# Row norms of q and k summed on the token side, and their inverse spread by TensorE, in a two-block transformer kernel

## The chip, the cores and the metric

The kernel runs on one core of a Trainium2 chip. The metric is the time of one execution in microseconds on the device; lower is better. The core has a matrix engine (TensorE, PE in the rows), a vector engine (VectorE, DVE), an activation engine (ScalarE, ACT), a general engine (GpSimd, POOL) and a queue that issues transfers (SyncE, SP). Each runs its own program, and they meet at semaphores.

## The reference, cut to what matters

The program is a stack of two blocks of two layers each, on 256 tokens of width 1024, all in float32. The first block (attention, memory attention, gated feed-forward) is not touched. Each of the two layers of the second block has a mixer, and in the mixer a gated delta rule with four heads of 128. Its queries and keys are normalised per token and head:

```python
def _l2norm(x):
    return x * lax.rsqrt(jnp.sum(x * x, axis=-1, keepdims=True) + EPS)
...
    qkv = jax.nn.silu(_dwconv(qkv, dn_conv)).astype(f32)
    q, k, v = _split(qkv, (DN_WIDTH, DN_WIDTH, DN_WIDTH))
    q = _l2norm(_to_heads(q, DN_HEADS)) * (DN_HEAD_DIM ** -0.5)
    k = _l2norm(_to_heads(k, DN_HEADS))
```

That is 2 (q, k) x 4 heads x 256 tokens = 2048 sums, each over 128 features.

## The kernel before, in words

**The stream of weights.** All weights pass through a ring of three slots of 1 MB each ("units"). ScalarE rounds each half of a unit to a high part (`w_hi`, 128x1024), VectorE subtracts to get the low part (`ring_lo`), and TensorE multiplies each unit in three passes (high x high, high x low, low x high). `feed(u)` on ScalarE and VectorE is the pair of halves of unit u+2; ScalarE may write a half of `w_hi` only when TensorE is done with the same half of unit u.

**The PSUM tiles.** Results that are not accumulated over a whole stage go into four banks, in a fixed order of tiles (class `Plan`). Tile t uses bank t modulo 4, and TensorE opens it (`open_tile`) only when tile t-4 has been read out. A tile's reader raises `tile_taken` of its bank.

**The mixer of layer l** (`mixer2`, once in each engine's program). TensorE first runs 18 units of projections (`PROJECTED`): q, k, v come out with features on the partitions and tokens along the row, in `qkvT`, 12 slabs of 128x256, of which slabs 0 to 3 are the heads of q and 4 to 7 those of k. ScalarE squares slabs 0 to 7 into `l2s` while the projection `hi` runs. Between the last unit of `hz` and the first of `z`, TensorE sums the squares: four matmuls with a matrix of ones as the stationary operand and 512 columns of squares moving, so that every partition receives the sum (tiles `l2`, four of them). Then it sums the decays (`decay_sums`, tile `gcum`, line 1115). ScalarE turns each of the four tiles into a 128x512 inverse root with Ln (line 1676) and Exp (line 1680) after loading the table for the two (line 1672), and VectorE multiplies q and k by it (line 2383). The units of `z` pass through Silu (line 1598).

**The loop of nine levels** (`for k in range(LEVELS + 2)`) follows. On TensorE a turn has the level's attention (eight matmuls, in turn 0 sixteen; tiles `level`), something extra (`prepare(k)`), and for k < 8 one unit `gate` of 48 matmuls on 256 columns. The extra is: k=0 and 1 the rows of the decays (`gcB0`, `gcB1`, eight matmuls each), k=2 the transposes of k and v to tokens on the partitions (`kv_T`, 16 of them), k=3 the products k x k (`G`, eight matmuls), k=4 the products q x k (`QK`, eight matmuls). On VectorE a turn is `gather` (reads the two level tiles, L2310 or L2313), its own `prepare`, `qmul` (L2296), `args` (L2273 and L2275) and `feed` of the gate unit (L1785 twice). On ScalarE it is `level_exp` (L1608), its `prepare` (at k=0 and 1 the decay matrices, L1697 and L1704), `feed` of the gate unit (L1314 twice) and the copy of the gate tile (L1279).

The order of instructions on each engine is the order in which the code is written; nothing is reordered.

Of the kernel before, what the change touches and what calls it, by code (L numbers as in the profile page):

```python
# [29 lines left out]
ALU = mybir.AluOpType  # L30
# [3 lines left out]
P = 128  # L34
# [34 lines left out]
PREP.update({0: (("gcB0", 2),), 1: (("gcB1", 2),), 2: (("kv_T", 4),), 3: (("G", 2),), 4: (("QK", 2),)})  # L69


class Plan:
# [104 lines left out]
    def stages(self):  # L177
# [287 lines left out]
def build(nc, weights, x_in, mem_in, consts, cols, ln_g_rows, ln_b_rows, gains, sink, rpb, hmask_in, wba_in, head_rows, decay_rows, final_norm,  # L465
          out):
    plan = Plan()
    with ExitStack() as ctx:
# [60 lines left out]
        def table(name):  # L529
# [36 lines left out]
                  "l2_sq", "l2_inv", "l2_done",  # L566
# [39 lines left out]
        l2_eps, ngc = small[:, 14, 0:2], small[:, 16, :]  # L606
# [90 lines left out]
        def _(pe):  # L697
# [375 lines left out]
            def mixer2(l):  # L1073
# [51 lines left out]
                def prepare(k):  # L1125
                    if k in (0, 1):
                        decay_rows_of(k)
                    if k == 2:
                        pe.wait_ge(sems["l2_done"], 4 * l + 4)
# [3 lines left out]
                    if k in (3, 4):  # L1133
                        for tt in range(TT):
                            per_head(T[("G" if k == 3 else "QK", l)] + tt, lambda h: qkvT[:, 4 + h, tt * P:(tt + 1) * P],
                                     lambda h: qkvT[:, (4 if k == 3 else 0) + h, tt * P:(tt + 1) * P])
# [129 lines left out]
        def _(act):  # L1266
# [323 lines left out]
            def mixer2(l):  # L1590
# [78 lines left out]
                for j in range(2):  # L1669
                    feed_one("hz", j)  # L1670
                    silu_tokens(T[("hz", l, j)], tok2(hz, j))
# [9 lines left out]
                for j in range(2):  # L1681
                    feed_one("z", j)
                    silu_tokens(T[("z", l, j)], tok2(zs, j))

                def prepare(k):
# [19 lines left out]
                    if k == 2:  # L1705
# [62 lines left out]
        def _(dve):  # L1768
# [561 lines left out]
            def mixer2(l):  # L2330
# [40 lines left out]

                t = T[("gcum", l)]
# [7 lines left out]
                feed_one("z", 0)  # L2380
                for j in range(4):
                    dve.wait_ge(sems["l2_inv"], 4 * l + j + 1)
                    V.tensor_tensor(pair(qkvT, j), pair(qkvT, j), pair(l2s, j), ALU.mult).then_inc(sems["l2_done"], 1)
                feed_one("z", 1)

                def prepare(k):
                    if k == 1:
                        dve.wait_ge(sems["gc_exp"], l + 1)
                        V.scalar_tensor_tensor(nbe, beta, -1.0, eg, ALU.mult, ALU.mult).then_inc(sems["nbe"], 1)
                    if k == 3:  # L2390
# [15 lines left out]
                    if k == 4:  # L2406
# [151 lines left out]
            step.did(V.tensor_scalar(l2_eps[:, 0:1], ident[:, 0:1], 0.0, P * EPS, ALU.mult, ALU.add))  # L2558
            step.link(V.tensor_scalar(l2_eps[:, 1:2], ident[:, 0:1], 0.0, EPS, ALU.mult, ALU.add))
# [132 lines left out]
```

## Time and profile before

| | us |
|---|---|
| median of 3 executions (2355.98 to 2367.64) | 2361.45 |
| the profiled execution | 2361.45 |
| its span from first to last instruction | 2359.7 |
| TensorE busy in the span | 2256.3 (96%) |
| VectorE busy | 1573.7 (67%) |
| ScalarE busy | 1075.8 (46%) |
| GpSimd busy | 151.3 (6%) |

The span is the time between the first and the last recorded instruction. Times in rows of a timeline are microseconds from its start. The mixer of layer 0 begins at about 1269 us, that of layer 1 at about 1811 us. The granted TensorE clock was 1.00 of full speed (2.4 GHz) between 1346 and 1470 us and between 1880 and 2012 us, the stretches in which the change lies. A float32 matmul shows as two records, each with a weight load of its own; a transpose shows as one.

### The profile page before, as it was taken

Reading aid. Unit: us, or ns where it says so; the run is one execution under the profiler, and the core shown is the slowest. Engines: PE = TensorE matmul, PEld = TensorE weight load, DVE = VectorE, ACT = ScalarE, POOL = GpSimd, SP = SyncE. Lnnn points to the kernel's source line nnn. Section 1 sums busy time; section 2 is a strip of 40 time slices with the busy share of each in tenths; the row PEclk is TensorE's granted clock in tenths of the full one; section 3 lists DMA queues with packets and bytes.
Section 4 is the critical chain, followed back from the end, with each engine's and each line's share of the span. In section 5 each row is a group of like instructions: output and inputs, shape, how many; then the busy total and the mean of one; then the engine's idle time right before and its main releaser. Section 6 shows DMA issues by size and latency. Waiting matters only on the chain.

```text
span 2359.7 us, 40274 instructions
## 1 busy us (share of the span) xinstructions
PE 2256.3 (96%) x16242; PEld 2105.1 (89%) x16242; DVE 1573.7 (67%) x2370; ACT 1075.8 (46%) x1524; POOL 151.3 (6%) x141
## 2 busy tenths in 40 slices
PE   7999889999999999999998998999999999899997
PEld 7998869989999998889997998998998999898996
DVE  4557747665665575756557878667767778567766
ACT  4335555433443455554333674334344575234432
POOL 0000000221000000000000011500000010500000
PEclk9999989999999999999999999999999999899999
DMA  7554414575555553435553433014554443014553
GB/s 260 182 192 170 152 54 161 169 220 182 206 195 188 180 194 126 142 145 179 187 186 130 161 126 108 1 72 161 189 184 161 161 143 120 7 42 164 190 185 124
DMA packets 52669, 359.75 MB, mean 152 GB/s; under 512 B 6400, under 2 KB 6784, under 8 KB 10944
## 3 DMA queue, kind: packets, MB, share of 16 engines
q1 hardware_dynamic: 46928, 340.81, 40.7%
q0 software_dynamic: 4336, 13.37, 1.9%
q10 hardware_dynamic: 1280, 3.77, 0.5%
q8 instruction: 95, 1.56, 0.3%
q14 instruction: 30, 0.25, 0.0%
HBM read 356.88 MB, written 1.05 MB: 152 GB/s over the span
## 4 chain that ended last, share of the span: by engine, by line
PE 83%; DVE 8%; ACT 4%; DMA 3%; issue 1%; POOL 0%; SPq 0%; POOLq 0%; DVEq 0%; ACTq 0%
PE tile L736 43%; PE acc L769 19%; PE tile L749 7%; PE tile L1060 6%; DMA ring<-weights 3%; PE tile L1243 2%; DVE ring_lo L1785 2%; ACT w_hi L1314 2%; PE tile L905 1%; PE tile L879 1%; PE tile L784 1%; PE tile L892 1%; DVE work L2467 0%; DVE bn L2170 0%; PE tile L710 0%
## 5 line engine op out<-in xcount | busy, mean ns | idle before, releaser
L1785 DVE TENSOR_TENSOR ring_lo<-ring,w_hi 128x1024 fp32r<-128x1024 f32 x648 | 782.1, 1238 | 605.1 <-ACT w_hi L1314 602.5
L1314 ACT ACTIVATE w_hi<-ring 128x1024 fp32r<-128x1024 f32 x648 | 657.5, 1053 | 887.8 <-DMA ring<-weights 722.1
L736 PE MATMUL tile<-xT_hi,w_hi 128*128 128x256 f32 x3008 | 856.1, 285 | 20.2 <-DVE xT_lo L1776 13.9
L736 PE MATMUL tile<-xT_lo,w_hi 128*128 128x256 f32 x3008 | 852.6, 283 | 0.0
L736 PE MATMUL tile<-xT_hi,ring_lo 128*128 128x256 f32 x3008 | 852.6, 283 | 0.0
L736 PEld LDWEIGHTS tile<-xT_hi,w_hi 128*128 128x128 f32 x3008 | 578.6, 192 | 27.7 <-DVE ring_lo L1785 12.7
L736 PEld LDWEIGHTS tile<-xT_lo,w_hi 128*128 128x128 f32 x3008 | 578.7, 192 | 2.1
L736 PEld LDWEIGHTS tile<-xT_hi,ring_lo 128*128 128x128 f32 x3008 | 578.6, 192 | 0.0
L769 PE MATMUL acc<-w_hi,hidden_hi 128*128 128x512 f32 x528 | 206.7, 391 | 3.1 <-DVE ring_lo L1785 3.1
L769 PE MATMUL acc<-w_hi,hidden_lo 128*128 128x512 f32 x528 | 206.1, 390 | 0.0
L769 PE MATMUL acc<-ring_lo,hidden_hi 128*128 128x512 f32 x528 | 205.5, 389 | 0.0
L1060 PE MATMUL tile<-work 128*128 128x128 f32 (+1 forms) x1568 | 191.5, 285 | 14.2 <-DVE work L2445 5.8
L1060 PEld LDWEIGHTS tile<-work 128*128 128x128 f32 x1568 | 187.8, 200 | 17.0 <-issue 9.3
L1279 ACT ACTIVATE work<-tile 128x512 f32<-128x512 f32 (+2 forms) x206 | 113.1, 570 | 128.4 <-PE tile L1060 87.9
L769 PEld LDWEIGHTS acc<-w_hi,hidden_hi 128*128 128x128 f32 x528 | 99.3, 188 | 23.0 <-issue 3.5
L769 PEld LDWEIGHTS acc<-ring_lo,hidden_hi 128*128 128x128 f32 x528 | 99.1, 188 | 21.1
L769 PEld LDWEIGHTS acc<-w_hi,hidden_lo 128*128 128x128 f32 x528 | 99.4, 188 | 18.3
L749 PE MATMUL tile<-w_hi,xT_hi 128*128 128x256 f32 x352 | 100.2, 285 | 7.2 <-ACT work L1585 3.2
L749 PE MATMUL tile<-w_hi,xT_lo 128*128 128x256 f32 x352 | 99.6, 283 | 0.0
L749 PE MATMUL tile<-ring_lo,xT_hi 128*128 128x256 f32 x352 | 99.6, 283 | 0.0
L2636 POOL TENSOR_TENSOR work<-work,levels 128x512 f32<-128x512 f32 x56 | 69.0, 1257 | 174.2 <-PE tile L1060 164.4
L769 PE MATMUL acc<-w_hi,xT_hi 128*128 128x512 f32 x192 | 77.6, 404 | 0.0
(254 smaller groups left out, 2681.9 us busy)
## 6 DMA issues: line engine op xcount, KB each, us to landing
ring<-weights SPq DMA_DIRECT2D x324, 1024.0 KB, 4.8
work<-ln_g_rows POOLq DMA_DIRECT2D x8, 512.0 KB, 5.0
work<-ln_b_rows POOLq DMA_DIRECT2D x8, 512.0 KB, 5.8
work<-rpb POOLq DMA_DIRECT2D x32, 96.0 KB, 14.3
work<-hmask_in ACTq DMA_DIRECT2D x1, 1408.0 KB, 9.8
x<-x_in SPq DMA_DIRECT2D x1, 1024.0 KB, 7.9
work<-mem_in ACTq DMA_DIRECT2D x1, 1024.0 KB, 6.7
out<-x POOLq DMA_DIRECT2D x1, 1024.0 KB, 4.4
```

The costliest lines, as they stand in the source:

```text
L736: j = mm(ps[:, f * S:(f + 1) * S], w[a][:, k, :], x2[b][:, k, :], start=(k == 0 and i == 0), stop=(k == KT - 1 and i == 2))
L749: j = mm(ps[:, tt * 256:(tt + 1) * 256], x2[b][:, k, tt * P:(tt + 1) * P], w[k // 4][a][:, k % 4, :], start=(k == 0 and i == 0), stop=(k = ...
L769: j = mm(acc[b][:, :], src[d][:, at + k, (b // 2) * P:(b // 2 + 1) * P], w[k][c][:, 0, (b % 2) * 512:(b % 2 + 1) * 512], start=(first and ...
L784: i = nc.tensor.transpose(ps[:, k * S + tt * P:k * S + (tt + 1) * P], src[:, tt, c:c + P], ident)
L879: i = mm(ps[:, tt * S:(tt + 1) * S], qs[m][:, tt * P:(tt + 1) * P], ks[m], start=(m == 0), stop=(m == len(qs) - 1))
L892: i = nc.tensor.transpose(ps[:, st * S + tt * P:st * S + (tt + 1) * P], prob[:, e % 6, tt, st * P:(st + 1) * P], ident)
L1060: i = mm(part(ps[:, h * P:(h + 1) * P]), lhsT(h), rhs(h), start=True, stop=True)
L1243: i = mm(ps[:, f * S:(f + 1) * S], w[c][:, k, f * P:(f + 1) * P], x2[d][:, 2 * q0 + k, :], start=(k + p == 0), stop=(k == 3 and p == 2))
L1279: A(dst, ps[:, :] if src is None else src(ps), ACT.Copy, scale=scale).then_inc(tile_taken[t % NB], 1)
L1314: A(high_of(u, h), half_of(ring, u, h), ACT.Copy).then_inc(sems["w_hi"], 1)
L1785: V.tensor_tensor(half_of(ring_lo, u, h), half_of(ring, u, h), high_of(u, h).bitcast(F32), ALU.subtract).then_inc(sems["w_lo"], 1)
L2636: G.tensor_tensor(heads2(alev[:, g, :]), heads2(amat[:, g, :]), mask.unsqueeze(1).to_broadcast([P, 4, P]), ALU.mult).then_inc(sems["a_leve ...
```

## The change

The sums are formed with the tokens on the partitions. The stationary operand is now a 128x128 block of squares (one head, 128 tokens) and the moving operand one column of ones, so that a matmul gives one column of 128 sums; 16 of them fill 16 columns of a single tile. VectorE adds EPS on the way out of PSUM (`l2_arg`), ScalarE takes the root of the 128x16 sums (`l2_sqrt`), and VectorE the reciprocal, with the factor of q (`l2_inv`). To multiply q and k, which lie the other way round, TensorE spreads each column over a tile: with the column, repeated 128 times, as the stationary operand and the identity moving, a matmul gives the 128 values as a row on every partition (tiles `l2B`, four tiles, 16 matmuls). This is the extra of turn k=2. The extras `kv_T`, `G` and `QK` move from turns 2, 3, 4 to turns 3, 4, 5 on all engines.

The plan, the tensor side, and the two others:

```diff
-PREP.update({0: (("gcB0", 2),), 1: (("gcB1", 2),), 2: (("kv_T", 4),), 3: (("G", 2),), 4: (("QK", 2),)})
+PREP.update({0: (("gcB0", 2),), 1: (("gcB1", 2),), 2: (("l2B", 4),),
+             3: (("kv_T", 4),), 4: (("G", 2),), 5: (("QK", 2),)})
...
-                    self.from_chip(("l2", l), 4)
+                    self.from_chip(("l2", l), 1)
...
                 def square_sums():
-                    for j in range(4):
-                        pe.wait_ge(sems["l2_sq"], 4 * l + j + 1)
-                        ps = open_tile(T[("l2", l)] + j)
-                        mm(ps[:, :], table("ones"), pair(l2s, j), start=True, stop=True).then_inc(sems["tile_ready"], 1)
+                    pe.wait_ge(sems["l2_sq"], 4 * l + 4)
+                    ps = open_tile(T[("l2", l)])
+                    for c in range(16):
+                        i = mm(ps[:, c:c + 1], l2s[:, c // 2, (c % 2) * P:(c % 2 + 1) * P], table("ones")[:, 0:1],
+                               start=True, stop=True)
+                    i.then_inc(sems["tile_ready"], 1)
...
                     if k == 2:
-                        pe.wait_ge(sems["l2_done"], 4 * l + 4)
+                        pe.wait_ge(sems["l2_inv"], l + 1)
                         for j in range(4):
+                            per_head(T[("l2B", l)] + j, lambda c: l2i[:, 4 * j + c:4 * j + c + 1].to_broadcast([P, P]),
+                                     lambda c: ident)
+                    if k == 3:
+                        pe.wait_ge(sems["l2_done"], l + 1)
...
-                nc.scalar.preload_act_table_set("natural_log_exp_and_others")
-                for j in range(4):
-                    t = T[("l2", l)] + j
-                    act.wait_ge(*ready(t))
-                    A(pair(l2s, j), bank[t % NB][:, :], ACT.Ln, bias=l2_eps[:, 0:1] if j < 2 else l2_eps[:, 1:2],
-                      scale=float(P) if j < 2 else 1.0).then_inc(tile_taken[t % NB], 1)
-                for j in range(4):
-                    act.wait_ge(*taken(T[("l2", l)] + j))
-                    A(pair(l2s, j), pair(l2s, j), ACT.Exp, scale=-0.5).then_inc(sems["l2_inv"], 1)
...
+                act.wait_ge(sems["l2_arg"], l + 1)
+                A(l2n, l2n, ACT.Sqrt).then_inc(sems["l2_sqrt"], 1)
...
+                t = T[("l2", l)]
+                dve.wait_ge(*ready(t))
+                V.tensor_scalar(l2n, bank[t % NB][:, 0:16], EPS, None, ALU.add).then_inc(tile_taken[t % NB], 1)
+                dve.wait_ge(*taken(t))
+                dve.sem_inc(sems["l2_arg"], 1)
...
-                    dve.wait_ge(sems["l2_inv"], 4 * l + j + 1)
-                    V.tensor_tensor(pair(qkvT, j), pair(qkvT, j), pair(l2s, j), ALU.mult).then_inc(sems["l2_done"], 1)
...
+                    if k == 0:
+                        dve.wait_ge(sems["l2_sqrt"], l + 1)
+                        step.link(V.reciprocal(l2i, l2n))
+                        V.tensor_scalar(l2i[:, 0:8], l2i[:, 0:8], float(P) ** -0.5, None, ALU.mult).then_inc(sems["l2_inv"], 1)
...
+                    if k == 2:
+                        for j in range(4):
+                            t = T[("l2B", l)] + j
+                            dve.wait_ge(*ready(t))
+                            V.tensor_tensor(pair(qkvT, j), pair(qkvT, j), bank[t % NB][:, :], ALU.mult).then_inc(tile_taken[t % NB], 1)
...
-            step.did(V.tensor_scalar(l2_eps[:, 0:1], ident[:, 0:1], 0.0, P * EPS, ALU.mult, ALU.add))
-            step.link(V.tensor_scalar(l2_eps[:, 1:2], ident[:, 0:1], 0.0, EPS, ALU.mult, ALU.add))
```

On TensorE, between the last unit of `hz` and the first of `z`, there stood (L749 are the units' matmuls, L1107 the sums of squares, L1115 and L1116 the decay sums):

```order
L749 MATMUL tile<-ring_lo,xT_hi 128x256
L1107 MATMUL tile<-l2s,const 128x512 x4
L1115 MATMUL tile<-small,const 128x4 x4
L1116 MATMUL tile<-small,const 128x16
L749 MATMUL tile<-w_hi,xT_hi 128x256
```

and there stands now:

```order
L750 MATMUL tile<-ring_lo,xT_hi 128x256
L1108 MATMUL tile<-const,l2s 128x1 x16
L1118 MATMUL tile<-small,const 128x4 x4
L1119 MATMUL tile<-small,const 128x16
L750 MATMUL tile<-w_hi,xT_hi 128x256
```

Four wide matmuls became 16 of one column, and the squares are now the stationary operand. On TensorE at turn k=2 of the loop there stood the level, the transposes (L1070) and the gate unit (L736):

```order
L736 MATMUL tile<-xT_hi,ring_lo 128x256
L1060 MATMUL tile<-work 128x128 x8
L1070 MATMUL tile<-const,work 128x128 x16
L736 MATMUL tile<-xT_hi,w_hi 128x256
L736 MATMUL tile<-xT_lo,w_hi 128x256
```

and there stands now:

```order
L737 MATMUL tile<-xT_hi,ring_lo 128x256
L1061 MATMUL tile<-work 128x128 x8
L1061 MATMUL tile<-const,small 128x128 x16
L737 MATMUL tile<-xT_hi,w_hi 128x256
L737 MATMUL tile<-xT_lo,w_hi 128x256
```

The 16 transposes are in turn 3 now, and 16 new matmuls are in their place. On ScalarE, from the end of unit `hz` to the first `level_exp` (L1598 is the Silu of hz and z, L1314 a half of the weights), there stood:

```order
L1598 ACTIVATE work<-tile 128x2x256
L1672 ACT_TABLE_LOAD
L1676 ACTIVATE l2s<-tile,small 128x512 x4
L1680 ACTIVATE l2s<-l2s 128x512 x4
L1314 ACTIVATE w_hi<-ring 128x1024 x2
L1598 ACT_TABLE_LOAD
L1598 ACTIVATE work<-tile 128x2x256
L1314 ACTIVATE w_hi<-ring 128x1024 x2
L1598 ACTIVATE work<-tile 128x2x256
L1608 ACT_TABLE_LOAD
L1608 ACTIVATE work<-work 128x2048
```

and there stands now:

```order
L1606 ACTIVATE work<-tile 128x2x256
L1322 ACTIVATE w_hi<-ring 128x1024 x2
L1606 ACTIVATE work<-tile 128x2x256
L1322 ACTIVATE w_hi<-ring 128x1024 x2
L1606 ACTIVATE work<-tile 128x2x256
L1682 ACT_TABLE_LOAD
L1682 ACTIVATE small<-small 128x16
L1616 ACT_TABLE_LOAD
L1616 ACTIVATE work<-work 128x2048
```

Eight wide activations and one of three table loads are gone; one small root stands between the last Silu and the first level's exponential. On VectorE, turn k=2 (L2312 is the gather, L2399 the multiplications of q and k, L2295, L2272 and L2274 are `qmul` and `args`, L1784 the halves of the weights) reads now:

```order
L2312 COPY_PREDICATED work<-hmask,tile 128x4x128 x2
L2399 TENSOR_TENSOR work<-work,tile 128x512 x4
L2295 TENSOR_TENSOR work<-work 128x1024
L2272 TENSOR_TENSOR work<-work 128x1024
L2274 TENSOR_TENSOR work<-work 128x1024
L1784 TENSOR_TENSOR ring_lo<-ring,w_hi 128x1024 x2
```

The four multiplications stood before the second half of `feed` of unit `z`, ahead of the loop.

## Rows read from the trace of the kernel before

**Rows 1.** The page: span, TensorE, and the chain that ended last.
```profile
span 2359.7 us, 40274 instructions
...
PE 2256.3 (96%) x16242; PEld 2105.1 (89%) x16242; DVE 1573.7 (67%) x2370; ACT 1075.8 (46%) x1524; POOL 151.3 (6%) x141
...
PE 83%; DVE 8%; ACT 4%; DMA 3%; issue 1%; POOL 0%; SPq 0%; POOLq 0%; DVEq 0%; ACTq 0%
```
**Rows 2.** Timeline, TensorE, sums of squares and decays: start, duration, records, [idle before].
```profile
1369.01 3.60 PE L1107 MATMUL tile<-l2s,const 128*128 128x512 f32 x8
1373.23 1.03 PE L1115 MATMUL tile<-small,const 128*128 128x4 f32 x8 [0.62 <-ACT l2s L1676]
...
1911.37 3.60 PE L1107 MATMUL tile<-l2s,const 128*128 128x512 f32 x8
1915.43 1.03 PE L1115 MATMUL tile<-small,const 128*128 128x4 f32 x8 [0.47 <-ACT l2s L1676]
1916.32 0.38 PE L1116 MATMUL tile<-small,const 128*128 128x16 f32 x2
```
**Rows 3.** Timeline, TensorE, the loop of layer 0 (turns 0 to 4, and its end).
```profile
1389.51 1.95 PE L1060 MATMUL tile<-const,small 128*128 128x128 f32 x16
1391.22 0.36 PE L736 MATMUL tile<-xT_hi,w_hi 128*128 128x256 f32 x1
...
1400.55 0.36 PE L736 MATMUL tile<-xT_hi,w_hi 128*128 128x256 f32 x1
...
1406.38 1.95 PE L1060 MATMUL tile<-work 128*128 128x128 f32 x16
...
1409.60 1.28 PE L1070 MATMUL tile<-const,work 128*128 128x128 f32 x8 [0.39 <-DVE work L2313]
...
1416.47 3.74 PE L1060 MATMUL tile<-work 128*128 128x128 f32 x32
1419.96 0.36 PE L736 MATMUL tile<-xT_hi,w_hi 128*128 128x256 f32 x1
...
1431.40 0.36 PE L736 MATMUL tile<-xT_hi,w_hi 128*128 128x256 f32 x1 [1.41 <-DVE work L2313]
...
1463.67 3.81 PE L1167 MATMUL tile<-work 128*128 128x128 f32 x32 [1.86 <-DVE work L2310]
```
**Rows 4.** Timeline, ScalarE, from the last Silu to the gate unit of turn 0.
```profile
1387.18 0.58 ACT L1598 ACTIVATE work<-tile 128x512 f32<-128x512 f32 x1
1387.78 1.28 ACT L1608 ACT_TABLE_LOAD   x1
1389.07 1.91 ACT L1608 ACTIVATE work<-work 128x2048 f32<-128x2048 f32 x1
1390.89 0.20 ACT L1688 ACTIVATE small<-small 128x16 f32<-128x16 f32 x1
...
1394.61 1.04 ACT L1314 ACTIVATE w_hi<-ring 128x1024 fp32r<-128x1024 f32 x1
1397.25 1.06 ACT L1314 ACTIVATE w_hi<-ring 128x1024 fp32r<-128x1024 f32 x1 [1.60 <-PE tile L736]
```
**Rows 5.** Timeline, VectorE, ahead of the mixer, ahead of the loop, and turns 0, 2, 5.
```profile
1258.11 0.15 DVE L2558 TENSOR_SCALAR small<-const 128x1 f32<-128x1 f32 x1 [0.23 <-DVEq L1930]
...
1258.36 1.29 DVE L2170 BATCH_NORM_STATS2 bn<-x 128x6 f32<-128x512 f32 x2
...
1382.62 2.49 DVE L2383 TENSOR_TENSOR work<-work,l2s 128x512 f32<-128x512 f32 x4
...
1398.34 1.23 DVE L1785 TENSOR_TENSOR ring_lo<-ring,w_hi 128x1024 fp32r<-128x1024 f32 x1 [1.29 <-ACT w_hi L1314]
...
1414.94 1.23 DVE L1785 TENSOR_TENSOR ring_lo<-ring,w_hi 128x1024 fp32r<-128x1024 f32 x1 [1.41 <-ACT w_hi L1314]
1417.76 1.23 DVE L1785 TENSOR_TENSOR ring_lo<-ring,w_hi 128x1024 fp32r<-128x1024 f32 x1 [1.59 <-ACT w_hi L1314]
...
1446.06 1.22 DVE L1785 TENSOR_TENSOR ring_lo<-ring,w_hi 128x1024 fp32r<-128x1024 f32 x1 [0.36 <-ACT w_hi L1314]
```

More of the change, by code:

```diff
@@ L605, in build @@
         note = small[:, 13, :]
-        l2_eps, ngc = small[:, 14, 0:2], small[:, 16, :]
+        l2n, l2i, ngc = [small[:, i, :] for i in range(14, 17)]
         ba32 = small[:, 0:2, :].rearrange("p a b -> p (a b)")
@@ L1668, in mixer2 @@
                     A(pair(l2s, j), pair(qkvT, j), ACT.Square).then_inc(sems["l2_sq"], 1)
-                for j in range(2):
-                    feed_one("hz", j)
-                    silu_tokens(T[("hz", l, j)], tok2(hz, j))
-                nc.scalar.preload_act_table_set("natural_log_exp_and_others")
-                for j in range(4):
-                    t = T[("l2", l)] + j
-                    act.wait_ge(*ready(t))
-                    A(pair(l2s, j), bank[t % NB][:, :], ACT.Ln, bias=l2_eps[:, 0:1] if j < 2 else l2_eps[:, 1:2],
-                      scale=float(P) if j < 2 else 1.0).then_inc(tile_taken[t % NB], 1)
-                for j in range(4):
-                    act.wait_ge(*taken(T[("l2", l)] + j))
-                    A(pair(l2s, j), pair(l2s, j), ACT.Exp, scale=-0.5).then_inc(sems["l2_inv"], 1)
-                for j in range(2):
-                    feed_one("z", j)
-                    silu_tokens(T[("z", l, j)], tok2(zs, j))
+                for name, dst in (("hz", hz), ("z", zs)):
+                    for j in range(2):
+                        feed_one(name, j)
+                        silu_tokens(T[(name, l, j)], tok2(dst, j))
+                act.wait_ge(sems["l2_arg"], l + 1)
+                A(l2n, l2n, ACT.Sqrt).then_inc(sems["l2_sqrt"], 1)
                 def prepare(k):
@@ L1704, in prepare @@
                             A(dec[:, g, :], dec[:, g, :], ACT.Exp, scale=-1.0).then_inc(sems["dec"], 1)
-                    if k == 2:
+                    if k == 3:
                         for j in range(4):
@@ L2379, in mixer2 @@
                 signal(sems["gc_arg"], 1)
-                feed_one("z", 0)
-                for j in range(4):
-                    dve.wait_ge(sems["l2_inv"], 4 * l + j + 1)
-                    V.tensor_tensor(pair(qkvT, j), pair(qkvT, j), pair(l2s, j), ALU.mult).then_inc(sems["l2_done"], 1)
-                feed_one("z", 1)
+                for j in range(2):
+                    feed_one("z", j)
                 def prepare(k):
+                    if k == 0:
+                        dve.wait_ge(sems["l2_sqrt"], l + 1)
+                        step.link(V.reciprocal(l2i, l2n))
+                        V.tensor_scalar(l2i[:, 0:8], l2i[:, 0:8], float(P) ** -0.5, None, ALU.mult).then_inc(sems["l2_inv"], 1)
                     if k == 1:
@@ L2389, in prepare @@
                         V.scalar_tensor_tensor(nbe, beta, -1.0, eg, ALU.mult, ALU.mult).then_inc(sems["nbe"], 1)
-                    if k == 3:
+                    if k == 2:
+                        for j in range(4):
+                            t = T[("l2B", l)] + j
+                            dve.wait_ge(*ready(t))
+                            V.tensor_tensor(pair(qkvT, j), pair(qkvT, j), bank[t % NB][:, :], ALU.mult).then_inc(tile_taken[t % NB], 1)
+                        for j in range(4):
+                            dve.wait_ge(*taken(T[("l2B", l)] + j))
+                        dve.sem_inc(sems["l2_done"], 1)
+                    if k == 4:
                         for tt in range(TT):
@@ L2405, in prepare @@
                             signal(tile_taken[t % NB], 1)
-                    if k == 4:
+                    if k == 5:
                         for tt in range(TT):
```

8 lines of the change are left out of this document (4 added, 4 removed).

## The prediction

> **What bounds the kernel now.** I read the page first. TensorE is busy for 2256.3 of 2359.7 us, and its own matmuls make up 83% of the chain that ended last [rows 1]. So a microsecond more of matmuls costs a microsecond, unless it falls into one of the few holes of that engine, and work taken from ScalarE or VectorE gains only where TensorE stood waiting for it. I then read the timeline of TensorE in the two stretches that the change touches. Between unit hz and unit z it runs the four wide sums of squares in 3.60 us, and then stands idle 0.62 us in layer 0 and 0.47 us in layer 1 until ScalarE's first Ln has emptied the bank that the decay sums need [rows 2]. In the loop of nine levels it is full but for three holes in layer 0: 0.39 us in the transposes of turn 2, 1.41 us before the gate unit of turn 4, and 1.86 us behind the loop, each ended by VectorE [rows 3]; layer 1 has the same three, of the same sizes within 0.01 us. Last I read ScalarE and VectorE at these places, for the slack that each has [rows 4, 5].
>
> **Sums of squares.** From their start to the start of the decay sums went 1373.23 - 1369.01 = 4.22 us in layer 0 and 1915.43 - 1911.37 = 4.06 us in layer 1. Now 16 matmuls of one column stand there, 32 records. No row has one column; the nearest has four: eight records took 1916.32 - 1915.43 = 0.89 us, 0.111 us each [rows 2]. With 128 columns 16 records took 1391.22 - 1389.51 = 1.71 us, 0.107 each [rows 3]. So going from 128 columns to 4 saves nothing: the pitch is at a floor that the 128x128 stationary operand sets. 32 x 0.111 = 3.56 us. Four times as many matmuls cost what the wide ones cost (8 x 0.45 = 3.60). What is saved is the idle time: the decay sums no longer wait for a Ln, since the single tile before them is emptied by VectorE and the bank that they use was free long ago. Layer 0: 4.22 - 3.56 = 0.66; layer 1: 4.06 - 3.56 = 0.50. Together -1.16 us. Bounds: at 0.107 a record it is -1.4. If so short matmuls did not overlap, each record would take the duration shown, 1.03 us less seven pitches, some 0.25 us: 32 x 0.25 = 8.0 us a layer, +7.8 in all instead of -1.16. I take the pitch, which is the measured one in a row of short matmuls.
>
> **Spreading the inverse.** 16 matmuls with 128 columns, 32 records, are new on TensorE in turn 2. In turn 3 the level's eight matmuls and the eight of G stand in one row of 32 records, and it took 1419.96 - 1416.47 = 3.49 us. The nearest row in kind, eight matmuls with a repeated column as stationary operand (gcB0), took 1.71, twice that is 3.42 [rows 3]. I take 3.49 a layer, 6.98 in all, with 6.8 to 7.8 as bounds (the upper by the full 1.95 us of a row of 16 records). Nothing hides it: it stands on TensorE between the level and the gate unit, and no row shows TensorE idle there.
>
> **A hole that comes with it.** The third l2B tile uses the bank of the level's first tile and so waits for VectorE's gather of turn 2, as the third transpose tile did, 0.39 us [rows 3]. Eight matmuls stand ahead of it now where eight transposes stood, and as rows they take 1.95 against 1.28 us, 0.67 more; but TensorE comes 0.66 us earlier, so it asks at the same time on the clock as before. If VectorE's gather comes 0.66 us earlier too, the hole is closed, and if not, it is 0.4 again; I put 0.2 a layer, 0.4 in all. The fourth tile, and the gate unit, which needs the first l2B tile multiplied, come behind it and are 0.6 us or more off.
>
> **What moves.** kv_T, G and QK are done one turn later. Turn 3 is what turn 2 was, with its 0.39; turn 4 what 3 was; turn 5 what 4 was, with its hole of 1.41. The hole comes from VectorE, which in the turn of G has more work than TensorE; it enters that turn from the same point, the second half of a feed, which ScalarE can start only when TensorE has ended the gate unit. After it there remain turns 6 to 8 to catch up, where there were 5 to 8. VectorE was waiting for ScalarE again, 0.36 us, at 1446.06, in the turn right after QK [rows 5], so I cost the move at nothing; if it were not back, the hole of 1.86 behind the loop would grow by what is left of 1.41.
>
> **VectorE.** The four multiplications (2.49 us [rows 5]) leave the stretch of unit z, where VectorE waited, and enter turn 2 between gather and qmul. In turn 2 VectorE waited 1.41 + 1.59 = 3.0 us for ScalarE's halves of the weights [rows 5], and TensorE's turn is now 3.5 us longer, so 6.5 us of cover stand over 2.5 us of work and a wait for the last l2B tile. Queued behind them are qmul and args of the next levels and the two halves of weights; TensorE asks for the first of these a gate unit later (1406.38 - 1400.55 = 5.83 us [rows 3]). Cost 0. If the cover failed, 2.5 us a layer would show as a later gather of turn 3. The two tiny constants ahead of the first mixer go: 1258.36 - 1258.11 = 0.25 us on a stretch where VectorE's chain leads to TensorE [rows 5]: -0.25.
>
> **ScalarE.** It loses eight wide activations and one of three table loads, and none of that was waited for but the first Ln. It gains a root right before the first level's exponential. Before, the last Silu ended at 1387.76 and the exponential began at 1389.07 [rows 4]. Now everything up to the Silu comes 0.66 us earlier, then load 1.28, root 0.20, load 1.28: the exponential starts at 1387.10 + 2.76 = 1389.9, 0.8 us later than before. The decay matrices behind it end at 1395.4 instead of 1394.6, and the first half of weights follows. The second half waits for TensorE's gate unit anyway (1397.25 before [rows 4]), which ends 0.66 us earlier, at 1396.4; ScalarE's first half ends at 1396.5. So ScalarE is back in step with TensorE at this point and the delay dies. Its second half ends at 1397.5; VectorE's, which ended at 1398.34 + 1.15 before [rows 5], ends at 1398.9, its gather of one tile 0.7 later at 1399.6, and TensorE wants that bank at 1400.55 - 0.66 = 1399.9 [rows 3]. Cost 0, with 0.3 us of slack.
>
> The Trainium skill sets a higher price on such a switch (ScalarE: Activation LUTs, What ACT_TABLE_LOAD costs): the load of 1283 ns is followed by a drain of 1380 ns, about 2.66 us for each change of set, and it advises against mixing Exp and Sqrt. The rows show the load, 1.28 us, and the exponential starting 1.29 us after the load started [rows 4], so no drain behind the load is seen here. By the page's figure the two switches would take 5.3 us and not 2.6; what that would do to TensorE is the third rival.
>
> **Sum.** 6.98 - 1.16 + 0.40 - 0.25 = +5.97 us on the profiled execution, whose own time, 2361.45, is also the median. Forecast: 2367.4 us, which is 0.25% more. A measurement of this kernel can tell about 0.5% (11.8 us) from no change, its three runs lying 11.7 us apart; so I forecast no change that can be told, with a lean to slower.
>
> **The rivals.**
> 1. *Short matmuls do not overlap* (slower). Place: the 16 sums of one column; price +7.8 instead of -1.16, so 2361.45 + 6.98 + 7.8 + 0.15 = 2376.4. It decides from a pitch of 0.23 us a record on, above which the sum passes 11.8. Against it: the 0.111 of the four-column row. For it: never 32 such records in a row were seen, and here the squares, not a small table, are stationary. Chance 0.06.
> 2. *The holes take the work in* (not slower). If the holes of TensorE behind turn 2 (0.39, 1.41, 1.86, together 3.66 a layer) are there because VectorE runs late in general, the 3.5 us that TensorE spends in turn 2 let VectorE get ahead and the holes shrink. All of them gone: 5.97 - 7.32 = -1.35, 2360.1. Against it: VectorE's lead is cut off each turn by a half of weights that waits for TensorE's gate unit (1.41 and 1.59 of waiting in turn 2 [rows 5]), so it can't run ahead. Chance 0.10.
> 3. *The switches of table cost twice as much.* The exponential comes 2.76 us later still; the first half of weights ends at 1399.2, the second at 1400.2, VectorE's half at 1401.4, its gather at 1402.1, where TensorE wants it at 1399.9: +2.2 a layer, 2371.8. Chance 0.04.
> 4. *VectorE's multiplications show in turn 2*: 2.4 us a layer, 2372.2. Against it: 6.5 us of cover. For it: GpSimd works in turns 0 and 1, and VectorE may be later than I carry it. Chance 0.10.
>
> **How the numbers follow.** The forecast, from about 2364 to 2371, has 0.65; the rivals 0.06, 0.10, 0.04, 0.10; 0.05 is left for something unseen, half of it on each side. The median of a few runs can lie 3 us off its centre, as the three runs show. Slower by over 0.5% (above 2373.3): the whole of rival 1, a third of rivals 3 and 4, and a little of the forecast and the unseen, 0.14. Faster by over 0.5% (below 2349.6): only the unseen, 0.02; all idle time that the change can reach is 8.5 us (7.32 in the loops and 1.09 in rows 2). The rest, 0.84, is within. The range 2359 to 2374 takes in rival 2, rivals 3 and 4, and leaves rival 1 out.
>
> **What would show it.** The decay sums start 3.5 to 3.6 us after the first sum of squares, with no idle time before them. TensorE's row in turn 2 holds 48 records in about 5.2 us, and the gate unit of that turn ends some 3 us later, relative to the first sum, than before. The hole of 1.41 stands before the gate unit of turn 5, that of 1.86 still behind the loop. ScalarE has a load, a root of 0.2 us, a load, at 1.3 us each. I would be wrong if the one-column records have a pitch above 0.2 us, if TensorE waits more than 0.5 us in turn 1, 2 or 3, or if the two mixers together are longer by less than 4 or more than 9 us.

## The result, and the profile after

| | before | after |
|---|---|---|
| median, us (12 executions each, side by side) | 2361.80 | 2376.07 |
| ratio after / before, 95% interval | | 1.0062 [1.0048, 1.0076] |
| lowest and highest of the 12, us | 2355.98, 2367.83 | 2373.01, 2381.92 |
| span of the profiled execution | 2359.7 | 2371.3 |
| both mixers, from the first sum of squares to the level of turn 8 (per layer) | 90.85 + 90.67 | 100.85 + 97.00 |

The change makes the kernel 14.3 us slower, where +6.0 was forecast (2367.4, range 2359 to 2374). The time is outside the range, and the forecast of no difference above 0.5% was wrong as well: it is 0.6%, for which the prediction had a chance of 0.14.

The two mixers are 16.3 us longer in the profiled execution, the span only 11.6. The rest of the difference lies in code that the change doesn't touch: from 200 to 400 us the granted clock was 0.99 in the execution of after and 0.93 in that of before, and after was 4.9 us ahead at its first sum of squares (1364.12 against 1369.01). Such differences come and go between executions of one kernel, so below each stretch is measured from a point inside the mixer. Each kernel has one profiled execution, with two layers in it.

Here is TensorE's timeline of after. Columns: start, duration, engine, line, operation, output and inputs, shapes, records, and in brackets the idle time before with what ended it.

```profile
1364.12 3.63 PE L1108 MATMUL tile<-const,l2s 128*128 128x1 f32 x32
1367.61 1.47 PE L1118 MATMUL tile<-small,const 128*128 128x4 f32 x8
1368.94 0.59 PE L1119 MATMUL tile<-small,const 128*128 128x16 f32 x2
...
1369.73 0.41 PE L750 MATMUL tile<-w_hi,xT_lo 128*128 128x256 f32 x1
1369.94 0.41 PE L750 MATMUL tile<-ring_lo,xT_hi 128*128 128x256 f32 x1
...
1376.17 0.28 PE L750 MATMUL tile<-w_hi,xT_hi 128*128 128x256 f32 x1
1376.29 0.28 PE L750 MATMUL tile<-w_hi,xT_lo 128*128 128x256 f32 x1
...
1383.37 3.74 PE L1093 MATMUL tile<-work 128*128 128x128 f32 x32
...
1397.71 1.16 PE L1061 MATMUL tile<-const,small 128*128 128x128 f32 x8 [0.39 <-ACT work L1287]
1400.63 0.36 PE L737 MATMUL tile<-xT_hi,w_hi 128*128 128x256 f32 x1 [1.76 <-DVE work L2312]
...
1407.94 1.95 PE L1061 MATMUL tile<-work 128*128 128x128 f32 x16
1409.73 3.74 PE L1061 MATMUL tile<-const,small 128*128 128x128 f32 x32
1413.22 0.36 PE L737 MATMUL tile<-xT_hi,w_hi 128*128 128x256 f32 x1
...
1444.07 0.36 PE L737 MATMUL tile<-xT_hi,w_hi 128*128 128x256 f32 x1 [1.41 <-DVE work L2312]
```

For comparison, level 0 and level 1 of layer 0 in before (TensorE), and a window of its unit z in the columns that are explained below:

```profile
1385.94 3.74 PE L1092 MATMUL tile<-work 128*128 128x128 f32 x32
...
1397.06 1.95 PE L1060 MATMUL tile<-work 128*128 128x128 f32 x16
```
```profile
1374.30:1385.90 11.60, 11.60 (x98) 11.60 (x98) 5.95 (x11) 7.23 (x10) 0.00 (x0) 1.00 0.26 93
```

Three things are to be seen. The decay sums start 1367.61 - 1364.12 = 3.49 us after the first sum, with no idle time before them; in [rows 2] it was 4.22 with 0.62 idle. Behind the sums, the matmuls of unit z are suddenly slower: one starts every 0.21 us and takes 0.41, until about 1375, and from then on one starts every 0.12 us and takes 0.28. And TensorE waits in turn 1, where before [rows 3] it did not. The same stretches by window say why (columns: window and its length, busy time and instructions of PE, PEld, DVE, ACT, POOL, then the granted clock, DMA share and GB/s):

```profile
1364.10:1368.00 3.90, 3.90 (x38) 3.90 (x36) 3.29 (x3) 1.93 (x3) 0.00 (x0) 1.00 0.61 206
1368.00:1370.00 2.00, 2.00 (x11) 2.00 (x12) 2.00 (x3) 0.00 (x0) 0.00 (x0) 0.51 0.29 123
1370.00:1374.00 4.00, 4.00 (x21) 4.00 (x21) 0.52 (x5) 0.00 (x0) 0.00 (x0) 0.50 0.00 0
1374.00:1376.00 2.00, 2.00 (x15) 2.00 (x15) 0.00 (x0) 0.00 (x0) 0.00 (x0) 0.78 0.00 0
1376.00:1383.40 7.40, 7.40 (x64) 7.40 (x64) 2.45 (x2) 2.61 (x3) 0.00 (x0) 1.00 0.42 144
...
1402.00:1406.00 4.00, 4.00 (x23) 4.00 (x22) 4.00 (x3) 1.91 (x3) 3.64 (x2) 0.57 0.00 0
...
1921.00:1923.00 2.00, 2.00 (x11) 2.00 (x11) 2.00 (x3) 0.00 (x0) 0.00 (x0) 0.50 0.05 21
1923.00:1925.00 2.00, 2.00 (x13) 2.00 (x13) 0.63 (x6) 0.00 (x0) 0.00 (x0) 0.65 0.00 0
```

During the one-column sums the clock is 1.00 (2.4 GHz). Right behind them it is 0.50 (1.2 GHz) for nearly 7 us, though TensorE is busy in every one of these windows from end to end. It falls once more behind the wait of turn 1. Layer 1 shows the first fall too, shorter (about 3.4 us), and not the second. In the execution of before the clock was 1.00 all through here.

ScalarE of after, from the last halves of z to the first turns (same columns):

```profile
1384.33 2.00 ACT L1322 ACTIVATE w_hi<-ring 128x1024 fp32r<-128x1024 f32 x2 [4.98 <-DMA ring<-weights]
1386.24 0.58 ACT L1606 ACTIVATE work<-tile 128x512 f32<-128x512 f32 x1
1386.84 1.28 ACT L1682 ACT_TABLE_LOAD   x1
1388.13 0.22 ACT L1682 ACTIVATE small<-small 128x16 f32<-128x16 f32 x1
1388.36 1.28 ACT L1616 ACT_TABLE_LOAD   x1
1389.66 1.91 ACT L1616 ACTIVATE work<-work 128x2048 f32<-128x2048 f32 x1
```

The first exponential starts 1389.66 - 1383.37 = 6.29 us after the level of turn 0 (5.41 in layer 1); before, it was 1389.07 [rows 4] less 1385.94 = 3.13. What hangs on it are GpSimd's masks (its multiplications of the decay matrices by a triangle of ones) and VectorE's halves of the weights:

```profile
1393.68 2.86 POOL L2635 TENSOR_TENSOR work<-work,const 128x512 f32<-128x512 f32 x1 [139.25 <-ACT work L1703]
1396.51 2.25 POOL L2635 TENSOR_TENSOR work<-work,const 128x512 f32<-128x512 f32 x1
```
```profile
1396.26 1.37 DVE L1784 TENSOR_TENSOR ring_lo<-ring,w_hi 128x1024 fp32r<-128x1024 f32 x1 [0.85 <-ACT w_hi L1322]
1397.55 2.29 DVE L1784 TENSOR_TENSOR ring_lo<-ring,w_hi 128x1024 fp32r<-128x1024 f32 x1
1399.77 1.33 DVE L2312 COPY_PREDICATED work<-hmask,tile 128x512 f32<-128x512 uint8 x2
```

The two halves take 1.37 and 2.29 us, together 3.58, instead of the 1.23 each of [rows 5]. Each began while a mask was running and ended 1.1 us behind that mask: the masks ended at 1396.5 and 1398.8, the halves at 1397.6 and 1399.8. TensorE's gate unit starts when the gather behind them has read its bank.

Where the time of a layer lies, in us, cut at the starts of TensorE's levels:

| stretch | before, layer 0 / 1 | after, layer 0 / 1 | difference | forecast |
|---|---|---|---|---|
| first sum to level of turn 0 | 16.93 / 16.77 | 19.25 / 17.73 | +2.32 / +0.96 | -0.66 / -0.50 |
| turn 0 | 11.12 / 11.11 | 11.11 / 11.11 | 0 / 0 | 0 |
| turn 1 | 9.32 / 9.33 | 13.46 / 11.12 | +4.14 / +1.79 | 0 |
| turns 2 to 7 | 53.48 / 53.46 | 57.03 / 57.04 | +3.55 / +3.58 | +3.69 / +3.69 |

The difference of layer 0 in turn 1 is 2.66 us of waiting and gaps, and 1.48 us by which its gate unit is longer.

So two steps failed, the sums of squares with what follows them and the slack of ScalarE in turn 1. The experiments take them apart.

### The profile page after: what moved, and what is told of

The parts are those of the page before. It is cut to its first block, busy times and chain, and to the rows that moved or that the text cites. A ratio compares the mean times of both kernels' runs of the same rounds, so it can differ in the third digit from the quotient of the medians.

```text
span 2371.3 us, 40480 instructions
## 1 busy us (share of the span) xinstructions
PE 2259.4 (95%) x16354; PEld 2116.9 (89%) x16354; DVE 1575.3 (66%) x2374; ACT 1063.9 (45%) x1508; POOL 150.6 (6%) x141
## 4 chain that ended last, share of the span: by engine, by line
PE 81%; DVE 9%; ACT 5%; DMA 4%; issue 1%; POOL 0%; SPq 0%; POOLq 0%; DVEq 0%; ACTq 0%
PE tile L737 43%; PE acc L770 18%; PE tile L750 6%; PE tile L1061 6%; DMA ring<-weights 4%; DVE ring_lo L1784 2%; ACT w_hi L1322 2%; PE tile L1251 2%; PE tile L906 1%; PE tile L880 1%; PE tile L785 1%; DVE work L2480 0%; DVE bn L2169 0%; DVE xT_lo L1775 0%; PE tile L711 0%
## 5 line engine op out<-in xcount | busy, mean ns | idle before, releaser
L1784 DVE TENSOR_TENSOR ring_lo<-ring,w_hi 128x1024 fp32r<-128x1024 f32 x648 | 781.4, 1237 | 615.8 <-ACT w_hi L1322 613.5
L1061 PE MATMUL tile<-work 128*128 128x128 f32 (+1 forms) x1568 | 191.5, 284 | 14.3 <-DVE work L2458 5.8
```

The costliest lines, as they stand in the source:

```text
L1061: i = mm(part(ps[:, h * P:(h + 1) * P]), lhsT(h), rhs(h), start=True, stop=True)
L1784: V.tensor_tensor(half_of(ring_lo, u, h), half_of(ring, u, h), high_of(u, h).bitcast(F32), ALU.subtract).then_inc(sems["w_lo"], 1)
```

## The experiments

"Turns" are named as above. The last table of this section has all numbers side by side.

**Is it the one column?** In after, the sums move 128 columns of ones instead of one; the same values are written, and the same stationary operands are loaded.

```diff
-    i = mm(ps[:, c:c + 1], l2s[...], table("ones")[:, 0:1],
+    i = mm(ps[:, c:c + P], l2s[...], table("ones"),
```

> The changed kernel, with the 16 sums of squares moving 128 columns of ones instead of one; each result is written to columns c to c+127 and overwritten from c+1 on, so that column c holds the same sum. Theory A (the stretch of one-column matmuls lets the granted clock of TensorE fall to 1.2 GHz, and unit z pays for it): the stretch itself keeps its 3.5 us, the clock stays at 1.00 through unit z, and from the first sum to the first level matmul layer 0 takes about 16.3 us instead of 19.25 and layer 1 about 16.3 instead of 17.7; the time is 4 to 7 us below the changed kernel, some 2370. Theory B (unit z is slow because of something else in the change, such as the weights arriving late or the decay sums): the fall of the clock stays where it is, and the wider operand changes nothing. Theory C (the wait in turn 1 has its own cause, ScalarE's later chain): its 1.5 to 1.8 us before the gate unit of turn 1 stay in both layers whatever the clock does.

```profile
1371.51 3.74 PE L1108 MATMUL tile<-const,l2s 128*128 128x128 f32 x32
1375.08 0.95 PE L1118 MATMUL tile<-small,const 128*128 128x4 f32 x8
```
```profile
1371.50:1376.10 4.60, 4.60 (x44) 4.60 (x43) 3.81 (x4) 2.12 (x3) 0.00 (x0) 1.00 0.64 228
1376.10:1387.70 11.60, 11.60 (x98) 11.60 (x98) 4.47 (x8) 2.61 (x3) 0.00 (x0) 1.00 0.25 93
```

These are TensorE's timeline and windows around its sums and unit z. The row takes 0.1 us more (3.57 to the decay sums, was 3.49), and unit z runs at 1.00 in 11.6 us. From the first sum to level 0 went 16.21 us in both layers: 0.72 and 0.56 less than before, which is the saving that was forecast (0.66 and 0.50). Against after it is 3.04 and 1.52 less. So theory A holds for the clock and theory B doesn't. The waits of turn 1 stay, as theory C had it (1.75 us, and 1.15 in layer 1, less than it said). Without a fall of the clock ahead of it, the wait of 1.75 had none behind it either. The whole kernel took 2372.80 us, 3.3 below after, where 4 to 7 was expected; its eight executions alone lie 9.4 us apart, so the cause is read from the stretches and not from this difference.

**The same in the old kernel.** To see that neither the squares nor the order of the work matter, before gets 16 matmuls more between its sums and its decay sums, identity stationary, ones moving, written to a bank that nobody reads then: of one column, and as a control of 128.

```diff
+    for c in range(16):
+        mm(acc[0][:, c:c + 1], ident, table("ones")[:, 0:1], start=True, stop=True)
```

> The kernel before, with 16 more matmuls that nothing reads, put between the sums of squares and the decay sums: stationary the identity, moving one column of ones, into an accumulator that is free there. Theory A: they take 3.5 us a layer, and in unit z that follows the granted clock falls to about half for some 3 to 6 us, which costs 1.5 to 3 us more a layer: +10 to +13 in all. Theory B: +7 in all, no fall of the clock. The idle time for the first Ln (0.62 and 0.47) is covered and gives back 1.1.

> The control of the one before: the same 16 matmuls in the same place with 128 columns moving. By every theory they take 3.5 us a layer, less the 0.5 of idle time that they cover: +6 in all, and the clock stays at 1.00 through unit z. The difference from the one-column kernel is the price of the clock.

```profile
1372.60:1376.10 3.50, 3.50 (x34) 3.49 (x32) 2.37 (x2) 3.50 (x7) 0.00 (x0) 1.00 0.28 119
1376.10:1377.70 1.60, 1.60 (x12) 1.60 (x12) 0.00 (x0) 0.79 (x2) 0.00 (x0) 0.68 0.00 0
1377.70:1383.00 5.30, 5.30 (x26) 5.30 (x27) 0.51 (x4) 0.00 (x0) 0.00 (x0) 0.50 0.00 0
```
```profile
1370.10:1374.20 4.10, 4.10 (x40) 4.10 (x38) 2.18 (x2) 4.09 (x8) 0.00 (x0) 1.00 0.22 94
1374.20:1386.20 12.00, 12.00 (x102) 12.00 (x102) 5.37 (x10) 4.33 (x5) 0.00 (x0) 1.00 0.25 89
```

The first three windows are of the kernel with one column, the last two of that with 128. Both rows of 32 records take the same time (3.49 and 3.57 us to the next row). Behind the one-column row the clock falls to 0.50, behind the other it stays at 1.00, and the price is 22.67 - 19.64 = 3.03 us in layer 0 and 21.12 - 19.64 = 1.48 in layer 1, within 0.05 of what it is in after. The medians are 11.2 and 7.1 us above before, where +10 to +13 and +6 were expected. So it is the one column alone, in either kernel.

In all, six layers have the row of 32 one-column records (after, late masks, and before with 16 more), and the clock fell in all six. Eight layers have it with 128 columns, and four have neither (before, and before with the extras moved): it was 1.00 through unit z in all twelve. In layer 1 of the kernel with late masks the fall came already within the row.

**Half the row at a time.** In after, eight one-column sums stand ahead of unit hz1 and eight behind it.

> The changed kernel with its 16 one-column matmuls cut in two halves, eight before the second unit of hz and eight behind it, so that no stretch of them is longer than 1.8 us. Theory A (the clock falls after a stretch of one-column matmuls): with half the stretch, followed by a full unit, the clock stays at 1.00 in both layers, unless the second eight together with the decay sums are enough; then it falls as before. If it stays, the time is that of wide sums, some 3 to 4 us below the changed kernel; the waits in turn 1 stay.

In layer 0 the clock stayed at 1.00 behind both halves, and unit z, behind the second, took 11.6 us:

```profile
1377.20:1388.70 11.50, 11.50 (x97) 11.50 (x98) 5.71 (x9) 2.61 (x3) 0.00 (x0) 1.00 0.40 153
```

In layer 1 it fell, and the unit took 13.1. The time was expected 3 to 4 us below after and was 2378.5 us, no faster than after. In the profiled execution the mixers were some 4.6 us shorter than in after, but the kernel was late already when it reached the first of them: about 3.6 us later than before, where after was 4.9 us ahead. One execution can't say how often a shorter row escapes; where the border lies stays open.

**Who makes TensorE wait in turn 1: the masks.** GpSimd starts its masks only when all four decay matrices are there (in after it takes them one by one):

```diff
-    pool.wait_ge(sems["dec"], 4 * l + g + 1)
+    pool.wait_ge(sems["dec"], 4 * l + 4)
```

> The changed kernel, with GpSimd's four masks of the decay matrices all started when the fourth matrix is ready, in place of two and two. Theory D (the wait of TensorE before the gate unit of turn 1 comes from VectorE's two halves of weights taking 3.58 us beside GpSimd's first two masks, in place of 2.36): the two halves take about 2.4 us, and the wait falls by 1.2 us, from 1.76 to about 0.5 in layer 0 and from 1.55 to 0.4 in layer 1. Rival E (the wait comes from ScalarE's chain alone, which starts its exponential 6.3 and 5.4 us behind the end of unit z instead of 3.1): the halves start when they do now and the wait stays over 1.2. The fall of the clock in unit z stays by either.

```profile
1399.47 1.16 PE L1061 MATMUL tile<-const,small 128*128 128x128 f32 x8 [0.30 <-ACT work L1287]
1401.17 0.35 PE L737 MATMUL tile<-xT_hi,w_hi 128*128 128x256 f32 x1 [0.54 <-DVE work L2312]
```
```profile
1398.02 2.36 DVE L1784 TENSOR_TENSOR ring_lo<-ring,w_hi 128x1024 fp32r<-128x1024 f32 x2 [0.86 <-ACT w_hi L1322]
```

These are TensorE and VectorE of that kernel in turn 1. The two halves are back at 2.36 us, and the wait for VectorE shrinks from 1.76 to 0.54 in layer 0 and is gone in layer 1. In layer 0 that is the 1.22 us by which the halves got shorter, as theory D had it. In layer 1, where 0.4 was expected, the weights of the next paragraph also landed 0.53 us earlier against level 0 than in after. The clock still falls behind the sums: it cost less in layer 0 than in after (17.73 us to level 0), and more in layer 1, where the fall began within the sums (4.74 us for the row, 20.87 to level 0). So the two mixers together are only 2.9 us shorter than in after.

**And the root.** The sums are wide, and ScalarE takes the root ahead of the units of z, not behind the last Silu. Its table load then falls into time in which ScalarE waits anyway.

```diff
                 for name, dst in (("hz", hz), ("z", zs)):
+                    if name == "z":
+                        act.wait_ge(sems["l2_arg"], l + 1)
+                        A(l2n, l2n, ACT.Sqrt).then_inc(sems["l2_sqrt"], 1)
...
-                act.wait_ge(sems["l2_arg"], l + 1)
-                A(l2n, l2n, ACT.Sqrt).then_inc(sems["l2_sqrt"], 1)
```

> The changed kernel with wide sums (128 columns moving), and with the root of the sums taken by ScalarE ahead of the units of z, where it waits for TensorE for over 7 us, in place of behind them; that adds one table load there (Sqrt, then Silu again). Theory F (the wait before the gate unit of turn 1, 1.75 and 1.15 us with wide sums, comes from the 1.5 us of table load and root between the last Silu and the first exponential): the exponential starts 1.5 us earlier relative to the end of unit z, about 4.4 us behind it, and the wait is at most 0.3 in both layers; the time falls by 2 to 3 us against wide sums alone. Rival G (the wait comes from the weights landing late, 6.1 us after their issue in layer 0 instead of 4.75): the exponential gains the 1.5, but where the weights land late the wait stays over 0.5.

```profile
1384.67 2.00 ACT L1322 ACTIVATE w_hi<-ring 128x1024 fp32r<-128x1024 f32 x2 [3.53 <-DMA ring<-weights]
...
1387.18 1.28 ACT L1616 ACT_TABLE_LOAD   x1
1388.47 1.91 ACT L1616 ACTIVATE work<-work 128x2048 f32<-128x2048 f32 x1
...
1932.31 2.00 ACT L1322 ACTIVATE w_hi<-ring 128x1024 fp32r<-128x1024 f32 x2 [2.33 <-DMA ring<-weights]
...
1936.11 1.91 ACT L1616 ACTIVATE work<-work 128x2048 f32<-128x2048 f32 x1
```

In before the row that answers to the first one reads:

```profile
1385.27 2.01 ACT L1314 ACTIVATE w_hi<-ring 128x1024 fp32r<-128x1024 f32 x2 [1.92 <-DMA ring<-weights]
```

ScalarE of the kernel with the early root: behind the Silu stands one load, not two with a root between. Level 0 starts at 1383.73 and 1932.58, so the exponential comes 4.74 and 3.53 us behind it. Layer 1 has no wait left, layer 0 still 0.88 us. So theory F holds in layer 1 alone, and layer 0 is as rival G said. The two mixers are 2.6 us shorter than with wide sums alone (2 to 3 expected); against before, each beside it, the medians say 4.2. What differs between the layers is the first row: the weights for which ScalarE waits landed 0.94 us after level 0 began in layer 0, and 0.27 before it in layer 1. In before ScalarE could start those halves at 1385.27, 0.67 ahead. The transfer is issued 5.4 us ahead of level 0 in before and in after alike; it took 4.75 and 4.81 us in before, 6.39 and 5.50 in after. It differs from one layer to the other of one execution (6.37 and 5.15 us here), but not by chance alone, it seems: in the eight layers of the four kernels built on the old one the weights landed 0.67 to 0.35 us before level 0, in the twelve layers of the six changed ones from 0.45 before to 1.02 after, and in eight of them after. Why wasn't tested and stays open.

**All three together** (wide sums, early root, late masks):

> Wide sums, early root and late masks together. What should be left of the change is what was forecast: 3.5 us a layer for the spreading less 0.5 to 0.7 for the idle time at the decay sums, about +3 a layer against the kernel before, with no fall of the clock in unit z and no wait in turn 1: 2366 to 2368. If turn 1 is free already with the early root, late masks gain nothing more and may cost VectorE time in turn 2.

Turn 1 is 9.33 us in both layers, as before the change, and the first stretch 16.20 and 16.21. In turn 2 of layer 1 one hole appears:

```profile
1952.02 1.95 PE L1061 MATMUL tile<-const,small 128*128 128x128 f32 x16
1954.56 0.71 PE L1061 MATMUL tile<-const,small 128*128 128x128 f32 x4 [0.59 <-DVE work L2313]
```

It stands after 16 of the 32 records of the spreading, before the third tile `l2B`, which waits for VectorE's gather. The late masks brought it, as the expectation feared. One of them began just before VectorE's second half of weights and held it, so that the half took 2.34 us and the gather began 3.55 us after the level; in layer 0 it began 2.43 after it:

```profile
1951.51 1.27 POOL L2636 TENSOR_TENSOR work<-work,const 128x512 f32<-128x512 f32 x1
```
```profile
1951.53 2.34 DVE L1785 TENSOR_TENSOR ring_lo<-ring,w_hi 128x1024 fp32r<-128x1024 f32 x1 [1.11 <-ACT w_hi L1322]
1953.79 1.33 DVE L2313 COPY_PREDICATED work<-hmask,tile 128x512 f32<-128x512 uint8 x2
```

The kernel takes 2367.8 us (2366 to 2368 expected), against 2362.05 of before beside it: +5.8, where the prediction said +5.97 for the change as it is. The ratio, 1.0026 [1.0013, 1.0040], leaves 3 to 9 us open; the mixers say +6.7, where +6.2 was forecast.

**The move alone.** In before, kv_T, G and QK go to turns 3, 4 and 5, and nothing else changes (`PREP` and the four conditions on k).

> The kernel before, with its sums of squares and its Ln and Exp untouched, and only the three extras kv_T, G and QK moved from turns 2, 3, 4 to 3, 4, 5; turn 2 has no extra. Forecast: no change (within 1 us), the hole of 1.41 us stands before the gate unit of turn 5, that of 1.86 behind the loop. Rival: VectorE has one turn fewer to catch up after QK, and the hole behind the loop grows; then it is up to 1.4 us a layer slower.

The mixers took 90.57 and 90.62 us, the ratio is 1.0008 [0.9992, 1.0024]. The holes of 1.41 (now in turn 5) and 1.86 (behind the loop) kept their sizes, and so did that of 0.39 (now in turn 3). No cost of the move shows.

All runs, in us. The mixers' sum is of the one profiled execution, the median is of 5 to 12, and the last column is the median less that of before, timed beside each. For the sums in halves the 5.83 us of unit hz1, which lies between them, are taken off:

| kernel | to level 0 | turn 1 | both mixers less before (181.52) | median | less before |
|---|---|---|---|---|---|
| after | 19.25 / 17.73 | 13.46 / 11.12 | +16.3 | 2376.07 | +14.3 |
| wide sums | 16.21 / 16.21 | 11.67 / 10.70 | +9.6 | 2372.80 | +11.6 |
| sums in halves | 16.13 / 17.61 | 12.04 / 11.11 | +11.7 | 2378.50 | +16.4 |
| late masks | 17.73 / 20.87 | 10.67 / 9.35 | +13.4 | 2373.31 | +12.1 |
| wide sums, early root | 16.21 / 16.21 | 10.44 / 9.33 | +7.0 | 2369.43 | +7.4 |
| all three | 16.20 / 16.21 | 9.33 / 9.33 | +6.7 | 2367.80 | +5.8 |
| before, 16 of one column more | 22.67 / 21.12 | 9.33 / 9.33 | +10.1 | 2372.34 | +11.2 |
| before, 16 of 128 columns more | 19.64 / 19.64 | 9.33 / 9.33 | +5.6 | 2368.25 | +7.1 |
| before, extras one turn later | 16.67 / 16.71 | 9.33 / 9.32 | -0.3 | 2364.02 | +2.0 |

The mixers' difference and that of the medians agree within 2.3 us, but for the sums in halves (4.8), whose single executions lie 16 us apart; those of the other kernels lie 5 to 13 us apart. No version is faster than before, which stays the best of all that ran.

## Why the prediction was wrong

**Sums of squares: the first step that failed.** Its pitch was right: 3.49 us for 32 records, 3.56 forecast, so rival 1 (short matmuls don't overlap) is false. The saved idle time was right too, as the wide sums show (1.28 us for both layers, 1.16 forecast). What the step left out is that the same row decides the clock of what comes behind it. It costed 16 matmuls by their own time alone. The decay sums and unit z behind them paid 3.04 and 1.52 us (after against wide sums). That the time of a row did not depend on its columns was taken as a reason that the columns don't matter; to the clock they did. The rival's price, 2376.4, is close to the result by accident, since its mechanism was absent. (Its threshold, a pitch of 0.23 us, comes out as 0.20 from the prediction's own terms; nothing hangs on it.)

**ScalarE: cost 0, with 0.3 us of slack: the second step that failed.** TensorE waited 0.39 + 1.76 us and 1.55 us in turn 1, and the prediction had named more than 0.5 us there as what would refute it. With the gaps that the split row leaves, the gate unit started 2.66 and 1.80 us late. The root with its load, 1.5 us, was in the chain as reckoned (2.76 for load, root and load, 2.82 measured). Two terms were put at nothing. First, the landing of the weights was taken as fixed: in layer 0 they landed 0.96 us after level 0 and not 0.67 before it, 1.63 us later (0.69 in layer 1), and all of ScalarE's chain moved with them. The step had ScalarE's second half wait for TensorE's gate unit and so fall back into step; in after it waited for nothing and ended 13.8 us after level 0, where 12.2 was reckoned. Second, GpSimd's masks were left out: the halves of VectorE met them now, and the second took 2.29 us, where 1.22 is what it takes alone. The trace of before already had such halves: one of 1.38 us in turn 0, and one of 2.31 in turn 1. Less the slack of 0.3 the two make 1.63 + 1.07 - 0.3 = 2.4 us in layer 0, where 2.66 was measured, and 0.69 + 1.07 - 0.3 = 1.5 in layer 1, where it was 1.80. These sums are worked out from the rows; the part of the masks is shown by an experiment, the part of the landing is not. The two remedies point the same way: with the masks alone moved, or with wide sums and the early root, layer 1 no longer waits for VectorE and layer 0 still does, 0.54 and 0.88 us; with all three neither waits, though in that execution the weights of layer 0 also landed 0.40 us before level 0.

**A cost on top, in layer 0.** Behind the wait of 1.76 us the clock fell again, and the gate unit took 7.31 us instead of 5.83, 1.48 more. Waits as long at the same place had none behind them: 1.75 us with wide sums, 1.77 with the sums in halves, 1.55 in layer 1. One execution alone shows the fall, and what decides it stays open.

**The hole in turn 2, put at 0.4 for both layers: 0 in after.** The prediction had two cases, that VectorE's gather moves along with TensorE or that it doesn't, and took the mean. It moved along: in layer 0 the gather began 2.43 us after the level in before and in after alike. The third transpose tile started 3.22 us after the level, 0.39 of it waiting; the third tile `l2B` is reached some 3.5 us after it, since eight matmuls take longer than eight transposes, and didn't wait. Nor did it in three layers in which TensorE came into turn 2 without a wait in turn 1 (layer 1 with late masks, layer 1 with the early root, layer 0 with all three). The 0.59 us in layer 1 of the kernel with all three repairs come from a late mask.

**Right:** the spreading, 3.49 us a layer; VectorE's four multiplications, hidden in turn 2 (rival 4 false, turn 2 is 11.1 us in both layers); the move (the experiment); the holes of 1.41 and 1.86, which kept their sizes (rival 2 false); and the switch of tables, where the root started 1.29 us after its load and the exponential 1.30 after its own, with no drain between (rival 3 false).

The account for the mixers, forecast +6.2, measured +16.3, outside the 4 to 9 us that the prediction allowed: clock behind the sums 4.56, waits and gaps in turn 1 4.46, second fall of the clock 1.48, hole in turn 2 -0.40. The sum of these is 10.1; what is left, 0.12 us more saved at the sums and 0.15 more spent in turns 2 to 7, comes to nothing.

## What to carry to other kernels

When a row of matmuls moves only one column, count not only its own time but look at the granted clock of what follows. If the pitch doesn't depend on the columns, pad the moving operand: here 128 columns cost 0.08 us more for 32 records and saved 3.04 and 1.52 us behind them. And where a step is said to have a slack of a few tenths, list everything that it takes as fixed, transfers and the engines off the chain too: GpSimd had 0% of the chain in [rows 1], and its masks cost TensorE 1.2 us in turn 1 of layer 0.

## What the runs showed of the hardware

The granted clock fell from 1.00 to 0.50 while TensorE was busy without a gap. In six layers of three kernels it did so behind, or in one of them within, a row of 32 records of one moving column (3.5 us); in eight layers of four kernels with 128 columns in the same row it stayed at 1.00 through the next unit. It came back by itself, after 3 to 10 us in which TensorE went on with its matmuls. The Trainium skill (TensorE: Matmul & The Clock Gate, Why this matters for your kernels) tells one to avoid idle gaps between bursts; here there was none, so that rule would have foreseen no fall, and the measurement decides.

Rows of 1, 4 and 128 columns have the same pitch, 0.109, 0.111 and 0.107 to 0.112 us a record. The Trainium skill (TensorE: Matmul & The Clock Gate, LDWEIGHTS (loading the stationary operand)) puts the load of the stationary operand at its columns divided by 1.2, in ns; by that, 128 columns are an estimated 107 ns, and the trace agrees within 0.005 us.

VectorE's tensor_tensor of 128x1024 on a half of the weights took 1.20 to 1.23 us where none of GpSimd's was running when it began. Of the halves in the ten traces, 178 began while a tensor_tensor of GpSimd had more than 0.1 us to run, and every one ended 1.08 or 1.09 us behind the end of that one. So what a mask costs depends on when the half begins: 1.37 us in all for one that began 0.3 us before the mask ended, 2.29 for one that began 1.2 us before it.
